# Loads of the experts' down weights issued by GpSimd instead of the sync engine

## What is computed

```python
logits = (xt @ w_router) + b_router                 # 256 tokens, 32 experts
top_val, top_idx = lax.top_k(logits, 4)
gates = jax.nn.softmax(top_val, axis=-1)
# for every expert e, on the tokens that chose it:
gu = xb @ w_gu[e] + b_gu[e]                         # w_gu[e]: 1024 x 2048
gate, lin = gu[:, :1024], gu[:, 1024:]
gate = jnp.minimum(gate, 7.0)
lin = jnp.clip(lin, -7.0, 7.0)
act = (lin + 1.0) * gate * jax.nn.sigmoid(1.702 * gate)
y = act @ w_down[e] + b_down[e]                     # w_down[e]: 1024 x 1024
```

## Time and profile before

| | us |
|---|---|
| median of 3 runs | 1188.95 (1187.77 to 1189.21) |
| the profiled execution, its own time | 1189.53 |
| its span, first to last instruction | 1187.7 |
| PE busy | 1147.3 (97%) |
| DVE busy | 327.9 (28%) |
| ACT busy | 206.1 (17%) |
| POOL busy | 30.9 (3%) |
| mean DMA rate over the span | 373 GB/s |

### The profile page before, as it was taken

How to read it: one execution, slowest core, us unless ns; L and a number is a source line. 1 busy time by engine, 2 the same in 40 slices (tenths; PEclk the granted TensorE clock), 3 DMA queues, 4 the chain that set the end, 5 groups by cost and what they waited for, 6 DMA issues and landing times.

```text
span 1187.7 us, 14555 instructions
## 1 busy us (share of the span) xinstructions
PE 1147.3 (97%) x5886; PEld 505.6 (43%) x5886; DVE 327.9 (28%) x568; ACT 206.1 (17%) x282; POOL 30.9 (3%) x27
## 2 busy tenths in 40 slices
PE   9999999999999999999999999999999999999997
PEld 5788999663333333333333333333333333223322
DVE  5697756332111111221111111111111111111112
ACT  3435433011101010101010101011110101010102
POOL 1050001100000000000000000000000000000000
PEclk9999999989999999999999999999999999999999
DMA  8873336888999999999999999999999999999994
GB/s 285 178 273 127 115 132 250 315 352 340 420 427 430 428 428 429 428 430 427 430 426 431 425 431 427 395 429 428 428 429 429 428 429 429 428 429 428 430 427 189
DMA packets 47628, 443.45 MB, mean 373 GB/s; under 512 B 4440, under 2 KB 8056, under 8 KB 23032
## 3 DMA queue, kind: packets, MB, share of 16 engines
q1 hardware_dynamic: 45832, 439.13, 89.6%
q10 hardware_dynamic: 1776, 4.04, 1.0%
HBM read 441.71 MB, written 1.44 MB: 373 GB/s over the span
## 4 chain that ended last, share of the span: by engine, by line
PE 61%; DMA 32%; DVE 4%; SPq 1%; issue 1%; ACT 1%; POOL 0%; POOLq 0%; DVEq 0%; ACTq 0%
PE psum L792 20%; DMA ring<-in_w_down 17%; PE psum L827 15%; DMA ring<-in_w_gu 13%; PE psum L751 3%; PE psum L766 3%; PE psum L724 2%; DMA ring<-in_w_in 2%; PE psum L467 2%; PE psum L462 2%; PE psum L463 2%; PE psum L803 1%; DVE slot_r L1054 1%; PE psum L570 1%; PE psum L760 1%; PE psum L814 1%
## 5 line engine op out<-in xcount | busy, mean ns | idle before, releaser
L792 PE MATMUL psum<-ring,hg 128*64 128x512 f32 x1280 | 289.5, 594 | 10.3 <-DMA ring<-in_w_gu 9.6
L827 PE MATMUL psum<-ring,hg 128*64 128x512 f32 x1024 | 233.9, 598 | 12.7 <-DMA ring<-in_w_down 12.7
L792 PEld LDWEIGHTS psum<-ring,hg 128*64 128x64 f32 x1280 | 89.9, 137 | 198.9 <-issue 179.1
L1320 DVE TENSOR_SCALAR hg<-psum 128x512 f32<-128x512 f32 x32 | 22.1, 692 | 398.5 <-PE psum L792 398.5
L827 PEld LDWEIGHTS psum<-ring,hg 128*64 128x64 f32 x1024 | 68.0, 136 | 134.0 <-issue 117.5
L990 ACT ACTIVATE hg<-hg 128x512 f32<-128x512 f32 x32 | 20.1, 629 | 415.9 <-DVE hg L1320 415.9
L1314 DVE TENSOR_SCALAR idx_region<-cst,tiny 128x128 f32 x64 | 19.3, 344 | 203.9 <-PE psum L827 202.5
L462 PE MATMUL psum<-hT_r,slot_r 128*128 128x256 f32 x288 | 72.9, 290 | 0.0
L463 PE MATMUL psum<-x_r,slot_r 128*128 128x256 f32 x288 | 71.4, 285 | 0.0
L751 PE MATMUL psum<-work,idx_region 128*64 128x512 f32 x264 | 71.0, 617 | 0.0
L766 PE MATMUL psum<-hg 64*128 64x512 f32 x264 | 65.6, 615 | 0.0
(11 more groups left out here) (252 smaller groups left out, 932.0 us busy)
## 6 DMA issues: line engine op xcount, KB each, us to landing
ring<-in_w_gu SPq DMA_DIRECT2D x80, 2048.0 KB, 26.1
ring<-in_w_down SPq DMA_DIRECT2D x64, 2048.0 KB, 21.9
bias_vb<-in_w_gu SPq DMA_DIRECT2D x16, 2048.0 KB, 24.5
qk_silu<-in_w_gu SPq DMA_DIRECT2D x16, 2048.0 KB, 29.3
sig_ab<-in_w_gu SPq DMA_DIRECT2D x16, 2048.0 KB, 28.0
ring<-in_w_in SPq DMA_DIRECT2D x11, 2048.0 KB, 8.5
ring<-in_w_out SPq DMA_DIRECT2D x2, 2048.0 KB, 14.0
ring<-in_w_up_a SPq DMA_DIRECT2D x1, 2048.0 KB, 8.6
```

Of the source, the lines that this page charges most:

```text
L792: last = mm(psum[half * 64:half * 64 + 64, b, :], xgT_sb[:, a:a + SLOTS], slot_gu(p, c, b, half)[:, jj], start=(j == 0), stop=(j == NJ - 1 ...
L827: last = mm(psum[half * 64:half * 64 + 64, 2, :], actT_sb[:, a:a + SLOTS], slot4(DOWN_HOME[c])[:, k, half * 512:(half + 1) * 512], start=( ...
L1320: v.tensor_scalar(gate_sb, psum[:, 0, :], LIMIT, None, ALU.min).then_inc(gate_ready, 1)
```

## The change

SP keeps the gu chunks; POOL gets `load_down` and `reload_down`, with the same waits ahead of each chunk, and issues them from its own queue. The down chunks of item 0 are issued behind POOL's wait for the last matmul of the merge (`merge_mm`), ahead of the two memsets; the others behind the two roots of the router's norm, in one loop for the items 1 to 17 and one by the table. The roots of the last norm come behind them.

```diff
--- before.py
+++ after.py
@@ block.sync
-            def load_down(e, c):
-                src = down_v[bass.ds(e, 1), :, 4 * c:4 * c + 4, :].rearrange("e p m n -> (e p) m n")
-                sp.dma_start(slot4(DOWN_HOME[c]), src).then_inc(down_loaded[c], 16)
-
             sp.wait_ge(o_mm, 1)
             load_gu(0, 0, 1)
             sp.wait_ge(w_used[slot_of(len(ORDER))], PRE_LOADS[slot_of(len(ORDER))])
             load_gu(0, 0, 2)
             load_gu(0, 0, 3)
-            load_down(0, 0)
             sp.wait_ge(w_used[slot_of(len(ORDER) + 1)], PRE_LOADS[slot_of(len(ORDER) + 1)])
-            load_down(0, 1)
             load_gu(1, 1, 0)
...
-            def reload_down(e, item):
-
-                sp.wait_ge(down_used, item)
-                load_down(e, 0)
-                sp.wait_ge(y_mm, item + 1)
-                load_down(e, 1)
-
             with sp.Fori(0, AHEAD // 2) as t:
                 reload_gu(t * 2 + 2, 0, t + 1)
-                reload_down(t * 2 + 1, t * 2 + 1)
                 reload_gu(t * 2 + 3, 1, t + 1)
-                reload_down(t * 2 + 2, t * 2 + 2)
-            reload_down(AHEAD + 1, AHEAD + 1)
             sp.wait_ge(table_ready, 1)
             n_trips = sp.value_load(...)
             with sp.Fori(AHEAD // 2 + 1, n_trips) as t:
                 for p in range(2):
                     e = sp.value_load(table[0:1, bass.ds(t * 2 + p, 1)], min_val=0, max_val=NE - 1)
                     reload_gu(e, p, t)
-                    reload_down(e, t * 2 + p)
@@ block.gpsimd
+            def load_down(e, c):
+                src = down_v[bass.ds(e, 1), :, 4 * c:4 * c + 4, :].rearrange("e p m n -> (e p) m n")
+                g.dma_start(slot4(DOWN_HOME[c]), src).then_inc(down_loaded[c], 16)
+
             pool.wait_ge(merge_mm, NJ)
+            load_down(0, 0)
+            load_down(0, 1)
             g.memset(y_sb, 0.0).then_inc(y_ready, 1)
             g.memset(combT_sb, 0.0).then_inc(combT_ready, 1)
...
             for r in range(NT):
                 pool.wait_ge(squares, NT + 2 * (r + 1))
                 mean_root(r, rs_ready)
+
+            def reload_down(e, item):
+
+                pool.wait_ge(down_used, item)
+                load_down(e, 0)
+                pool.wait_ge(y_mm, item + 1)
+                load_down(e, 1)
+
+            with pool.Fori(0, AHEAD + 1) as i:
+                reload_down(i + 1, i + 1)
+            pool.wait_ge(table_ready, 1)
+            n_trips = pool.value_load(table[0:1, 2 * TAB:2 * TAB + 1], min_val=NE // 2, max_val=MAX_ITEMS // 2)
+            with pool.Fori(AHEAD // 2 + 1, n_trips) as t:
+                for p in range(2):
+                    e = pool.value_load(table[0:1, bass.ds(t * 2 + p, 1)], min_val=0, max_val=NE - 1)
+                    reload_down(e, t * 2 + p)
             for r in range(NT):
                 pool.wait_ge(final_ss, 2 * (r + 1))
                 mean_root(r, final_rs)
```

## The result

After: 1193.29 us in the median of 7 runs (1192.13 to 1194.17), against 1188.71 (1186.33 to 1189.21) of the kernel before, run beside it: ratio **1.0044 [1.0034, 1.0054]**, slower by 4.6 us by the medians (the interval of the ratio is 4.0 to 6.4 us). The forecast was 5.5 us slower. The profiled execution took 1194.17 us, its span is 1192.5; the other six lie lower, down to 1192.13.

A forecast was written before the change was run, and what follows sets the result against it. The DMA engines were taken to bound the expert loop. The profiled 1189.53 us plus 5.5 for who is last (-2.2 gap included, issues and first loads 0) gave 1195.0, less 0.58 for the median 1194.5 us; range 1186.5 to 1204.

The forecast's parts named there:

- The bound: Expert loop: DMA engines limit it at 29.38 us per item, 428 GB/s; TensorE is faster by 1.84 us per item.
- The gap, -2.2 us: Load order switch at item 18: DMA falls to 333 GB/s from 740 to 750 us; two queues close it, -2.2 us.
- POOL's issues and the first loads, 0 us: 64 DMA issues moved to POOL, taken as 1 us each, and item 0's down loads: no cost, 0 us.
- The far case: Item 0's two down issues ahead of the root at 235.46: over 7.8 us each, the excess delays routing.
- The queues take turns packet by packet, half each: DMA engines alternate one packet per queue, so POOL's down gets half the rate and overtakes gu.
- Down's median near 10 us: Sign in the profile: down chunks land about 10 us after issue in the median instead of 21.9.
- Who is last, +5.5 us: End of loop: gu ends last instead of down, with 16.3 us of TensorE work behind; +5.5 us, the -2.2 included.
- All three cases: End of loop: gu very last, +7.6 us; equal turns after a wait at item 30, +3.2, or one item earlier, +5.2.
- The case with a wait at item 30 (+3.2): Equal turns, TensorE having waited for gu 3 of item 30: item 31's gu ends 4.4 us before DMA's end; +3.2 us.
- Rates (1 and 2): All transfers run faster with two queues (8.9 us per 1%, chance 0.08) or slower (1% gives 1203.4, chance 0.11).
- Down starves (3): POOL's queue gets clearly under a third, TensorE waits for down: +25 to +45 us, 1214 to 1234; chance 0.10.
- Nothing overtakes (4): Transfers run in order of issue and only the gap closes: 1186.8 us; chance 0.11.

The follow-up runs named there:

- e2: Changed kernel, but POOL loads down only for items 0 to 17 and SP, in the earlier order, for items 18 to 31: 1187.53 us, ratio 0.9999.
- e8: Changed kernel with each down chunk of POOL cut into four DMAs with rows of 4 KB instead of one of 16 KB: 1271.07 us, ratio 1.0736.
- e5: Changed kernel, but ACT instead of POOL issues down of items 1 to 31 from its own queue, SP item 0's: 1194.29 us, ratio 1.0050.
- e4: Changed kernel, but for items 30 and 31 POOL issues down only once gu chunk 3 of the same item has landed: 1197.81 us, ratio 1.0090.

## Why the prediction was right, and where only in part

**The bound.** Right. The loop's rate is 427 GB/s before and 428 after, and 817 us of TensorE work in 840 did not matter to it.

**The gap, -2.2 us.** Right in kind, too large. DMA's end came 1.4 us earlier by the two windows, 1.6 after correcting for the start, and e2, which has this gain alone, is 1.0 us shorter than before. The rate in the gap was averaged over 10 us and read to a few per cent, so a term of 2.2 was known to about half a microsecond at best.

**POOL's issues and the first loads, 0 us.** Right: 0.53 us each against 1 us taken, and the root 0.14 us later. The far case, an issue long enough to delay the root, is real: e8 reached it.

**The queues take turns packet by packet, half each.** Right, and the foundation of the rest. It was read from eight small transfers in the earlier trace rows; after shows 83 packets against 84, e8 240 against 240, and e5 the same 14.4 us from ACT. "Down's median near 10 us" was too low: the first down chunk of item 30, issued at 1118.94, took 14.0 us, and I had not counted the time before its bytes begin to move. The DMA view from 1118.9 to 1122.5 us has packets of SP's queue alone:

```profile
q1 hardware_dynamic: 96, 1.52, 99.2%
```

The first packets of POOL's queue move at 1122.7 us, 3.7 us behind the issue, and the last end at 1131.8, 9.1 us later (9.8 would be exactly half the rate); 1.1 us after that the chunk has landed. The Trainium skill, DMA: Bandwidth & Descriptors, section Queues, rings and completion order, has each DMA engine go round between the queues that have work, a packet at a time; by that rule, the trace agrees. The Trainium skill, DMA: Bandwidth & Descriptors, section Issuing engines are not separate DMA queues, says that starting DMAs from several engines saves only their issue time. For the rate this is what the trace shows (428 against 427 GB/s), but the order in which chunks land changed, and that cost 4.6 us, the slow group behind the last wait included.

**Who is last, +5.5 us.** The right size, from parts that were not all right. All three cases took gu chunk 3 of item 31 as the last wait. It was that of item 30; item 31's had landed 2.4 us before it was wanted. The case with a wait at item 30 (+3.2) did not ask when TensorE itself comes to item 31's chunk. With six chunks behind it, gu chunk 3 of item 30 is seen at 1166.3 - 29.4 + 1.9 = 1138.8, and 27.54 us later, at 1166.3, TensorE wants item 31's, which that case has ready at 1163.8. So TensorE's own work bounds the end, and the case should have given +5.7. The runs differ from that in two terms. Not 6 but 6.7 chunks lay behind gu chunk 3 of item 30, since down chunk 1 of item 30 was still on its way; so that chunk was seen at 1136.1, and 43.8 us of work behind it give a loss of 3.1 us. The other 1.7 us are the slow group behind the wait, a term that the sum does not have. The late start of POOL's bytes helped item 31's gu chunk to be early. I had leaned towards +5.5 by an argument about rarer waits; the number is near the 4.8 of the trace, but not for that reason. So it is in part luck that the sum came near, and wholly luck that 3.1 stands next to the 3.2 of that case.

**Rivals.** Rates (1 and 2): excluded by 428 against 427 GB/s in the loop. The Trainium skill, DMA: Bandwidth & Descriptors, section Latency and other measured facts, has DMA engines 7 and 15 slower with GpSimd's descriptors; no view here shows single DMA engines, but neither the mean rate nor down's landing time (14.4 us by POOL and by ACT) shows a cost. Down starves (3): not in after, but real, and reached by e8 with shorter rows, at 83 us instead of 25 to 45, 11.8 of them ahead of the loop. Nothing overtakes (4): excluded by the landing times.

**Steps of the forecast profile.** A chain through gu and none through down: the ten waits are all for gu and none for down, though the chain itself runs 90% through TensorE. No gap near 745: so. DMA's end near 1166: 1167.1. The last gu chunk seen 3 to 8 us later than 1160.60: item 31's was used 4.85 us later, but it was TensorE that was late, not the chunk.

## What to carry to other kernels

When the DMA engines bound a loop, as here at 427 and 428 GB/s, a change of who issues a load does not make the loop faster; it changes the order in which loads land. The time is DMA's end plus the work behind the last wait less the transfers behind the chunk waited for. Count both, and ask at each later chunk whether the chunk or TensorE comes last. So read the end of the trace first: the load with the most work behind it must come first there, and one in-order queue is a way to say so. A second queue gets its turn packet by packet, and a wait ahead of its issue cannot give it back its place (e4).

## What the runs showed of the hardware that was not expected

- TensorE ran slow right behind some waits for DMA. A group of 16 matmuls took 5.35 us instead of 3.65 behind waits of 2.37 us (1136.14) and 3.58 us (843.08), with a granted clock of 0.50 from 1138 to 1140 us and 1.00 in the wait itself. It is not the wait's length alone: behind 2.33 us (724.98) and 2.38 us (783.73) in the same trace, and behind 2.97 us (1164.05) in e5, the group took 3.65.
- Two queues share by packets and not by bytes: 83 against 84 with equal rows of 16 KB, 240 against 240 with rows of 4 KB against 16 KB, which left the shorter ones 21% of the bytes.
- A DMA issue takes POOL 0.53 us in after. With four in a row for one chunk the last was often held, 4.54 us at 830.12 in e8, and the last of eight in a row 26.67 us.
- The first bytes of a POOL load began to move 3.7 us behind its issue while SP's queue had work (1118.94 to 1122.7); those of ACT's in e5 3.5 us (1117.49 to 1120.96).
